# Four square-root norms, earlier x tiles, later row broadcasts and fewer waking matmuls at the start of a hybrid layer

## What is computed

```
h = rmsnorm(x, g_mix);  proj = h @ w_in            # 1024 -> 512 a | 512 u | 512 v | 1024 gate_a | 1024 gate_b
u, v = gelu(u), rmsnorm(gelu(v), g_v)
pa = pool_mixer(a)                                 # trailing means over 2, 4, 8, 16 tokens, minus a
s  = (causal 128x128 matrix per group) @ v + b_s   # inside chunks of 128 tokens
x  = x + (sigmoid(gate_a) * (pa @ w_pool_out) + sigmoid(gate_b) * (u*s @ w_gmlp_out)) @ w_out
x  = x + (silu(h2 @ w_gate) * (h2 @ w_up)) @ w_down,   h2 = rmsnorm(x, g_ffn)
y  = rmsnorm(x, g_final)
rmsnorm(x, g) = x / sqrt(mean(x*x) + 1e-6) * g
```

## Time and profile before

| | us |
|---|---|
| median of 3 runs | 763.07 (762.78 to 763.62) |
| the profiled execution | 763.88 |
| its span, core 5 (the slowest) | 762.2 |
| spans of the eight cores | 755.2 to 762.2 |
| TensorE busy | 740.2 (97%) |
| DVE, ACT, POOL busy | 545.3, 354.1, 108.9 |
| mean granted TensorE clock, all cores | 0.994 to 0.995 |

### The profile page before, as it was taken

One profiled execution on the slowest core, in us unless ns is written; L12 is line 12 of the kernel. 1 busy time (PEld: TensorE's weight loads), 2 busy tenths in 40 slices (PEclk: granted clock), 3 DMA queues, 4 the chain that ended last, 5 costly groups with the idle time before them and its releaser, 6 DMA issues.

```text
span 762.2 us, 14673 instructions; the slowest of 8 cores (755.2 to 762.2 us)
## 1 busy us (share of the span) xinstructions
PE 740.2 (97%) x4811; PEld 436.5 (57%) x4811; DVE 545.3 (72%) x1099; ACT 354.1 (46%) x752; POOL 108.9 (14%) x192
## 2 busy tenths in 40 slices
PE   8989999999999999998999999999999999999995
PEld 4644454666666664444666666666666654445542
DVE  3699987777777665776767676767667698766664
ACT  4496445454445545665555555555555510111111
POOL 5143322000000001212011010000001300000000
PEclk9999999999999999999999999999999999999998
DMA  8993449221313248757995232323233770633322
GB/s 186 230 277 60 69 60 144 36 42 30 42 29 43 56 124 250 111 99 124 233 247 104 43 43 43 55 32 53 43 43 43 99 192 1 221 111 127 123 101 96
DMA packets 53501, 77.45 MB, mean 102 GB/s; under 512 B 28721, under 2 KB 29233, under 8 KB 53410
## 3 DMA queue, kind: packets, MB, share of 16 engines
q0 software_dynamic: 15840, 28.84, 25.7%
q1 hardware_dynamic: 37150, 47.36, 21.1%
q10 hardware_dynamic: 436, 0.31, 0.1%
HBM read 82.03 MB, written 17.40 MB: 130 GB/s over the span
## 4 chain that ended last, share of the span: by engine, by line
PE 88%; DVE 5%; issue 2%; ACT 2%; DMA 2%; POOL 0%; DVEq 0%; ACTq 0%; POOLq 0%
PE ps L475 85%; DMA hT<-wpk 2%; PE ps L1286 1%; ACT junk L497 1%; DVE actr L507 1%; PE ps L986 1%; DVE ring L507 1%; DVE hT L507 1%; DVE hb L512 1%; DVE X L507 1%; PE ps L765 1%; POOL rs L625 0%; ACT Fb L497 0%; PE ps L658 0%; DVE Fb L507 0%
## 5 line engine op out<-in xcount | busy, mean ns | idle before, releaser
L475 PE MATMUL ps<-hT,ring 128*128 128x384 f16 (+6 forms) x1428 | 230.9, 311 | 4.3 <-ACT Fb L497 1.8
L507 DVE TENSOR_TENSOR Fb<-Fb,ps 128x344 f32<-128x344 f32 (+3 forms) x299 | 154.2, 530 | 51.7 <-ACT Fb L497 24.4
L475 PEld LDWEIGHTS ps<-hT,ring 128*128 128x128 f16 x1428 | 133.1, 99 | 83.0 <-issue 7.6
L497 ACT ACTIVATE Fb<-ps 128x384 f32<-128x384 f32 (+5 forms) x245 | 114.7, 474 | 117.6 <-PE ps L475 93.2
L497 ACT ACTIVATE Fb<-Fb 128x384 f32<-128x384 f32 (+2 forms) x174 | 85.9, 494 | 76.8 <-DVE Fb L507 74.9
L507 DVE TENSOR_TENSOR X<-X,ps 128x512 f32<-128x512 f32 (+6 forms) x157 | 83.9, 545 | 46.6 <-PE ps L475 25.9
L475 PE MATMUL ps<-actr,ring 128*128 128x344 f16 (+2 forms) x600 | 108.7, 309 | 0.8 <-ACT X L497 0.8
L531 POOL DMA_DIRECT2D ring<-wpk x93 | 49.6, 543 | 308.0 <-PE ps L475 292.7
L625 POOL TENSOR_TENSOR rs<-ss,mhalf 128x1 f32<-128x1 f32 (+1 forms) x67 | 48.6, 727 | 261.4 <-ACT junk L497 255.8
L475 PE MATMUL ps<-ring,mrg 128*128 128x512 f16 x360 | 81.4, 379 | 0.0
L475 PEld LDWEIGHTS ps<-actr,ring 128*128 128x128 f16 x600 | 57.4, 98 | 31.1 <-issue 1.1
(11 more groups left out here) (173 smaller groups left out, 781.1 us busy)
## 6 DMA issues: line engine op xcount, KB each, us to landing
ring<-wpk POOLq DMA_DIRECT2D x93, 256.0 KB, 4.6
X<-xp SPq DMA_DIRECT2D x25, 512.0 KB, 8.9
x1d<-X SPq DMA_DIRECT2D x16, 512.0 KB, 12.7
Fb<-x1d SPq DMA_DIRECT2D x8, 512.0 KB, 4.0
yp<-Fb SPq DMA_DIRECT2D x8, 512.0 KB, 2.7
hT<-wpk POOLq DMA_DIRECT2D x8, 256.0 KB, 12.4
actr<-x1d SPq DMA_DIRECT2D x4, 512.0 KB, 3.3
X<-x1d SPq DMA_DIRECT2D x4, 512.0 KB, 4.0
```

The lines of the kernel that those rows point to most:

```text
L475: ins = e.matmul(out=ap, lhsT=l, rhs=rr, start=(start and i == 0), stop=(stop and i == len(pairs) - 1), skip_group_check=skip)
L497: return e.activation(out=P.r(out), in_=P.r(in_), func=func, scale=scale, **kw)
L507: return P.add(eng, lambda e: e.tensor_tensor(out=P.r(out), in0=P.r(a), in1=P.r(b), op=op), reads=[a, b], writes=[out], dur=vdur(n, per), ...
```

## The change

Four things change, all in the code of the first 125 us.

- The norms of tiles 0 to 3 get their factor by a square root on ACT and a reciprocal on DVE (root) in place of the power on POOL. The first instruction of ACT is a square root, so that its table is the first one loaded, and a one-element gelu (table) stands behind the last of the four roots.
- x tiles 4 and 5 wait for v 1, tile 6 for v 2, tile 7 for v 3; u 0 to 3 now wait for x tiles 4 to 7. Tile 8 waits for u 1, tiles 9 to 11 for u 2.
- The matmuls that spread g_v and b_s get a margin of 17 us in the plan, so that they come later. The identity is loaded ahead of the first gain row on ACT's queue, and small ACT loads are booked as landing 3.5 us after their issue.
- Bank 7 is free from 34 us on; waking matmuls are put in up to 31 us, and in gaps that begin before 5 us one stands for each 430 ns. There were 12, 12, 2, 3 and 3 of them; now there are 4, 10, 2, 10 and 4.

```diff
@@ Prog.schedule
+                if o.eng == 'act' and o.nbytes < 16384:
+                    lead, tail = 0.0, o.end + 3500.0 - dma_free
@@ loads
+        dma('act', ident_f[:, :], cst[:, C_ID:C_ID + 128], 'c0', 65536, -10.1)
         dma('act', grow[0:1, 0:1024], rowc[:, 0:1024], 'c1', 8192, -10)
-        dma('act', ident_f[:, :], cst[:, C_ID:C_ID + 128], 'c0', 65536, -9)
+        for t, u in ((4, ('v', 1)), (5, ('v', 1)), (6, ('v', 2)), (7, ('v', 3))):
+            xload(t, after=[wd_[u]])
         for g in range(4):
-            wd_[('u', g)] = load_unit(('u', g), 4 + g, 0.3 + 0.01 * g)
+            wd_[('u', g)] = load_unit(('u', g), 4 + g, 0.3 + 0.01 * g, [x_dma[4 + g]])
-        xg = {4: ('v', 3), 5: ('u', 0), 6: ('u', 1), 7: ('u', 2)}
-        for t in range(4, 12):
-            xload(t, after=[wd_[xg.get(t, ('u', 3))]])
+        for t in range(8, 12):
+            xload(t, after=[wd_[('u', 1 + (t > 8))]])
-        act(stmp[:, 0:1], mhalf[:, 0:1], AF.Square, -8.5)
+        memset('dve', scr[:, :], 1.0, -8.6)
+        act(stmp[:, 0:1], scr[:, 0:1], AF.Sqrt, -8.5)
-            mm(pt, lambda p: p[:, :], [(ones1[0:1, :], grow[0:1, 512 * j:512 * j + 512])], pr)
+            mm(pt, lambda p: p[:, :], [(ones1[0:1, :], grow[0:1, 512 * j:512 * j + 512])], pr,
+               margin=0.0 if j < 2 else 17000.0)
@@ norms
+        def root(k, R, prio):
+            r = rs[:R, k:k + 1]
+            s_ = P.add('act', lambda e: e.activation(out=r, in_=ss[:R, k:k + 1], func=AF.Sqrt), ...)
+            P.add('dve', lambda e: e.reciprocal(out=r, in_=r), ...)
+            return r, s_
-            r = rstd(X[:R, XR(t), 0:D + 1], R, 1.0 / 32.0, prio, 600.0 if two else 0.0)
+            r = rstd(X[:R, XR(t), 0:D + 1], R, 1.0 / 32.0, prio, 600.0 if two else 0.0, sq=t < 4 and not two)
+        table(AF.Gelu_apprx_tanh, last_sqrt[0], -3.0, 2500.0)
@@ waking matmuls
-        P.schedule([0.0] * 7 + [50000.0])
+        P.schedule([0.0] * 7 + [34000.0])
-            if o_.start < 45000.0:
+            if o_.start < 31000.0:
-                n_ = int((gap - 200.0) / 235.0) if gap > 700.0 else 0
+                n_ = int((gap - 200.0) / (430.0 if t_ < 5000.0 else 235.0)) if gap > 700.0 else 0
```

15 lines of the change are left out of this document (11 added, 4 removed).

## The result

| | us |
|---|---|
| kernel before, median of the runs beside it | 763.07 |
| changed kernel, median of 7 runs | 768.54 (lowest 767.28) |
| ratio of the changed kernel to the one before | 1.0066, 95% interval 1.0052 to 1.0080 |
| its profiled execution, span, slowest core | 767.91, 766.3, core 4 |
| spans of its eight cores | 756.5 to 766.3 |

The change makes the kernel 0.66% or 5.0 us slower. (The ratio compares undisturbed executions; two of the seven, 790.85 and 905.66 us, ran with some cores at a lower clock and are left out of it.) The predicted time was 762.5 with a range up to 765.2; the sign was wrong, and the range missed it.

What follows compares the result with a forecast made beforehand. TensorE, busy for 97% of the span, was taken as the bound. Terms -4.0 + 1.9 + 1.0 + 0.8 - 0.3 summed to -0.6 us, so 763.07 became 762.5 us, with a range from 760.2 to 765.2.

Steps and rivals of the forecast that it cites:

- The bubbles: TensorE's idle time at tiles 4 to 7, 40.54 to 49.19 us: earlier x tiles remove it, -4.0 us.
- Later u weights: Loads of u 0 to 3 behind x tiles 4 to 7: still in time for TensorE, slim cover, 0 us.
- a wait on ring from a DMA before the u products: Sign in TensorE's timeline before the u products: it would mean that the u weights are late.
- The spatial products: Spatial matmuls at 68.68 us: their 0.34 us wait for DVE goes, as that work is now behind it, -0.3 us.
- Everything later keeps its order and moves as one: Everything behind the spatial matmuls at 68.68 us: claimed to shift together, with no term of its own.
- The head: Start up to tile 3's transposes: tile 3 at 22.5 instead of 21.52 us, +1.0, bounds -0.1 and +2.6.
- Rival B: Head: ACT's order and lower clock cost more, tile 3 at 25.1, +3.6 there, 765.1 us in all; chance 0.12.
- The second spreading: Moved behind the last a products, where nothing covers it: +1.9 us, bounds 1.7 and 2.0.
- some tenths: Head chain: worth of the clock staying up through 18 to 20 us, some tenths of a us.
- VectorE in the packed stretch: DVE's list before hb of tiles 4 and 5: TensorE waits 0.3 and 0.5 us, +0.8, bounds 0 and 2.
- The roots and the table: Norms of tiles 0 to 3: quick roots whose gain ACT's order eats; gelu table load of 1.28 us hidden.
- rival C: x tiles 4 to 7 land no earlier, since loads share the engines: bubbles stay, about +3, 766 us; chance 0.08.

Runs made afterwards that it cites:

- b1_loads: Kernel before with only x tiles 4 to 7 loaded ahead of the u weights: 764.79 us, ratio 0.9996.
- b8_scaling: Kernel before with x tiles 4 to 7 ahead of the u weights and v tile 7's scaling one hb product sooner on VectorE: 763.83 us, ratio 0.9981.
- b8_again: Second run, in more rounds, of the kernel before with early x tiles and v tile 7's scaling one hb product sooner: 763.28 us, ratio 0.9977.
- e1_pool_first: Changed kernel with the loads of u 1 to 3 right behind u 0 on GpSimd's list, ahead of the powers: 766.23 us, ratio 1.0038.
- e5_four, All four moves: Changed kernel with u loads first, gain row first, tile 1's square one place up and v tile 7's scaling one product sooner: 765.69 us, ratio 1.0010.
- e4_three: Changed kernel with u loads ahead of the powers, gain row ahead of the identity and tile 1's square one place up: 764.85 us, ratio 1.0024.
- e6_vtok: Changed kernel with only v tile 7's scaling one hb product sooner on VectorE's list: 770.26 us, ratio 1.0059.
- e2_row_first: Changed kernel with the first gain row ahead of the identity on ScalarE's queue: 766.0 us, ratio 1.0035.
- e7_spread_back: e5_four with the second spreading and its two copies back ahead of tile 1's transposes, replacing ten waking matmuls: 766.46 us, ratio 1.0012.
- b4_roots: Kernel before with only the first four norms by square root and reciprocal, and the Gelu table load: ratio 0.9984.
- the fifth: e5_four with the power of tile 4 ahead of the load of u 3 on GpSimd's list: 765.65 us, ratio 1.0007.

## Why the prediction was wrong

**The bubbles, -4.0 us: right in mechanism, and not all of it is a gain.** Tile 4 was to be asked for at 35.5 and was transposed at 36.5 on average, 1 us later because the head was; the idle time between tiles is 0.35 us. Alone (b1_loads) the loads bring tile 4 to 34.0. But with the wait before spatial 1 they gave nothing at the gates beyond 0.4 us, and without most of it 0.7 and 1.2 (b8_scaling, b8_again), 0.2% of the time. Since the wait for the delayed transpose still stands there (1.69 us), what is late next seems to be the chain over ScalarE, GpSimd and VectorE between 50 and 75 us, which no run isolates; the prediction had named VectorE's hb as late next, and only up to tile 5.

**"Later u weights: 0": the step that failed.** I took the release of each load (the landing of tiles 4 to 7, "u 3 at 34 to 37") and the time that TensorE asks for it, and called the cover slim. The landing was in time: u 0 went out at 29.04. What I left out is that these loads are items of GpSimd's list, and that the planner now sets them between the powers of tiles 4 to 6, whose squares ScalarE makes late (u 3 was issued at 38.60, not at 34 to 37, and took 10.5 us, not 8.9). I had read the changed lists of ScalarE and TensorE, and not those of GpSimd and VectorE, where both surprises stand. The price measured: a wait of 2.68 us and 1.7 us of lower clock on the slowest core, 2.1 us of time (e1_pool_first). The sign that I had named for it, a wait on ring from a DMA before the u products, is in the rows.

**The spatial products, -0.3: wrong sign.** I reckoned that VectorE would be done with its work behind a later TensorE. It was the other way: the last v tile's factor came 0.9 us later relative to TensorE than before, and the list had a pooling sum and an hb product still to come ahead of its scaling. The wait was 1.88 us instead of 0.34, with the lower clock behind it on four cores. "Everything later keeps its order and moves as one" was the sentence that hid it; VectorE's list does not keep its order there. Taken away with a single move it pays little, since the hb product is needed too (e5_four 0.14% under e4_three, both intervals wide; e6_vtok 0.07% under the changed kernel).

**The head, +1.0 with bounds -0.1 and +2.6: mis-sized.** It measured +2.1 (tile 3). The first spreading began at 5.84 on core 4 (5.03 to 6.30 on the eight cores) against my 5.3, it took the 3.75 us forecast for the lower level, and of the ten waking matmuls some eight ran at that level (3.88 us, at 0.438 and 0.230 each), against my five and 3.3 us. From tile 0 to tile 3 I had worked out 10.2 us, and core 4 shows 13.23 to 23.41, 10.2. The gain row's place explains most of it (e2_row_first: 1.2 us back at tile 3, 2.4 in time, more than the head's part; where the rest came back the runs don't show). Rival B had the slow waking matmuls, with 3.6 us for the head.

**The second spreading, +1.9: its own 1.98 us are there (27.68), what the move costs on balance is open.** The old place has a price as well, the lower clock behind it: it brings tile 3 1.3 us later in e7_spread_back. The earlier trace rows had shown that clock at 18 us, and I had counted it with "some tenths". But six waking matmuls in the place that the spreading left, and the wait for tile 4, keep that run from telling the difference.

**VectorE in the packed stretch, +0.8:** a wait of 0.35 us before tile 5, the same on every core, and none before tile 4; within its bounds. **The roots and the table:** as forecast, the load costs 1.28 us and is hidden, and the roots alone do no harm (b4_roots). The Trainium skill's figure of 2.66 us with a drain ("ScalarE: Activation LUTs", "What ACT_TABLE_LOAD costs") is not what these rows show. The load runs from 24.73 to 26.01, the activation ahead of it ends at 24.72 and the next one begins at 26.03, so there is no room for a drain.

Together, from -0.6: the late weights +2.1 by e1_pool_first, the wait before spatial 1 +1.8 (1.88 - 0.34 instead of -0.3), the head +1.1: +4.4 of the 5.1 us at the gates. What is left is about what the lower clock behind spatial 1 costs on the mean of the cores (0.14 of 12 us on four of eight: 0.8 us), which no term of the sum held. These parts overlap, so the sum is a rough one: in e1_pool_first only one core falls behind spatial 1, not four, and the 2.1 us hold that too. The measured time lies beyond rival C's 766 as well, though its condition did not come about: tile 4 had landed by 29.04, before the 31.3 of the forecast. All four moves together bring the changed kernel to 1.0010, and to 1.0007 with the fifth, no longer told from no change, where the sum without side effects had -0.6 us. The rival theory, that the new parts as such cost the time, falls for the roots (0.9984 alone) and for the x tiles (0.9996 alone); for the spreading's new place it stands open.
